# A fused two-block transformer kernel: order of gated products, sums, splits and row broadcasts

## The reference

```
h = rms_norm(x, norm1_g);  z = h @ w_in          # parts for three mixers and three gates
y = sigmoid(g_m)*(hm @ p_m) + sigmoid(g_a)*(ha @ p_a) + sigmoid(g_r)*(hr @ p_r)
x = x + y @ w_out
x = x + (silu(h2 @ w_gate) * (h2 @ w_up)) @ w_down
```

## Time and profile before

| | us | share of the span |
|---|---|---|
| median of 3 runs | 1624.04 | |
| profiled execution, span | 1618.2 | |
| TensorE (PE) busy | 1532.6 | 95% |
| weight loads (PEld) busy | 1163.6 | 72% |
| GpSimd (POOL) busy | 1261.5 | 78% |
| ScalarE (ACT) busy | 715.2 | 44% |
| VectorE (DVE) busy | 696.8 | 43% |

### The profile page before, as it was taken

How to read it: one execution, slowest core, us unless ns; L and a number is a source line. 1 busy time by engine, 2 the same in 40 slices (tenths; PEclk the granted TensorE clock), 3 DMA queues, 4 the chain that set the end, 5 groups by cost and what they waited for, 6 DMA issues and landing times.

```text
span 1618.2 us, 21936 instructions
## 1 busy us (share of the span) xinstructions
PE 1532.6 (95%) x7018; PEld 1163.6 (72%) x7018; DVE 696.8 (43%) x1306; ACT 715.2 (44%) x879; POOL 1261.5 (78%) x1509
## 2 busy tenths in 40 slices
PE   7989999999999999989999998999999899999996
PEld 5767877788887777777788776878785656646634
DVE  3986844300127986844210036355544122122215
ACT  4544543544446544534544445546341422325323
POOL 7997898999999996969999997977591634529713
PEclk9999999999999999999999999998999999999998
DMA  6654454677765553445677664645364988899990
GB/s 223 214 176 117 132 157 141 195 217 220 216 199 169 165 155 106 143 133 153 203 212 214 183 220 133 186 140 166 92 204 144 350 331 323 340 382 398 396 363 39
DMA packets 95525, 333.83 MB, mean 206 GB/s; under 512 B 11136, under 2 KB 15760, under 8 KB 94384
## 3 DMA queue, kind: packets, MB, share of 16 engines
q1 hardware_dynamic: 88240, 307.26, 58.1%
q10 hardware_dynamic: 6048, 21.22, 3.8%
q0 software_dynamic: 1152, 4.19, 0.7%
HBM read 322.12 MB, written 21.00 MB: 212 GB/s over the span
## 4 chain that ended last, share of the span: by engine, by line
POOL 53%; PE 27%; issue 15%; DMA 2%; DVE 1%; ACT 1%; POOLq 1%; ACTq 0%; DVEq 0%; SPq 0%
POOL w_lo L1835 52%; PE bank L671 7%; PE bank L1178 6%; PE bank L1232 3%; PE bank L1175 3%; PE bank L1198 3%; PE bank L1248 2%; PE bank L1288 1%; DMA logits<-outputs_by_expert,tiny 1%; DMA arena<-in_experts 1%; POOL w_lo L1842 1%; ACT w_hi L1402 1%; POOLq L1830 1%; PE bank L1218 0%; PE bank L1073 0%
## 5 line engine op out<-in xcount | busy, mean ns | idle before, releaser
L1835 POOL TENSOR_TENSOR w_lo<-raw,w_hi 128x256 fp32r<-128x256 f32 x1416 | 1067.6, 795 | 139.0 <-ACT w_hi L1402 138.0
L671 PE MATMUL bank<-w_hi,hT 128*128 128x512 f32 x2240 | 716.2, 401 | 39.4 <-POOL w_lo L1835 11.8
L1402 ACT ACTIVATE w_hi<-raw 128x1024 fp32r<-128x1024 f32 x371 | 393.0, 1059 | 545.6 <-DMA raw<-in_stream 291.0
L671 PEld LDWEIGHTS bank<-w_hi,hT 128*128 128x128 f32 x2240 | 417.4, 191 | 142.5 <-POOL w_lo L1835 19.9
L671 PE MATMUL bank<-w_lo,hT 128*128 128x512 f32 x1120 | 443.3, 396 | 0.0
L671 PEld LDWEIGHTS bank<-w_lo,hT 128*128 128x128 f32 x1120 | 213.9, 191 | 47.3
L1842 POOL TENSOR_TENSOR w_lo<-arena,w_hi 128x1024 fp32r<-128x1024 f32 x61 | 144.6, 2385 | 129.8 <-ACT w_hi L1402 129.7
L982 PE MATMUL bank<-w_hi,mixT 128*128 128x512 f32 x352 | 109.9, 393 | 1.0 <-POOL w_lo L1835 1.0
L671 PE MATMUL bank<-w_hi,mixT 128*128 128x512 f32 x288 | 91.6, 399 | 3.9 <-POOL w_lo L1835 2.6
L1402 ACT ACTIVATE w_hi<-arena 128x1024 fp32r<-128x1024 f32 x61 | 63.9, 1057 | 59.4 <-PE bank L1178 31.1
L2246 DVE SCALAR_TENSOR_TENSOR arena<-bank,tiny,arena 128x256 f32<-128x256 f32 x44 | 21.1, 483 | 155.5 <-ACT arena L1558 143.0
(11 more groups left out here) (392 smaller groups left out, 1928.3 us busy)
## 6 DMA issues: line engine op xcount, KB each, us to landing
raw<-in_stream SPq DMA_DIRECT2D x357, 512.0 KB, 3.6
arena<-in_experts SPq DMA_DIRECT2D x154, 512.0 KB, 11.1
raw<-in_experts SPq DMA_DIRECT2D x38, 512.0 KB, 9.5
rows_by_expert<-in_blank ACTq DMA_DIRECT2D x56, 128.0 KB, 3.3
arena<-in_stream SPq DMA_DIRECT2D x9, 512.0 KB, 13.2
gates<-rows_by_expert SPq DMA_DIRECT2D x3, 1024.0 KB, 7.7
outputs_by_expert<-xn ACTq DMA_DIRECT2D x3, 1024.0 KB, 8.4
bias_skewed<-bias_windows SPq DMA_DIRECT2D x4, 512.0 KB, 4.8
```

The costliest lines, as they stand in the source:

```text
L671: mm = pe.matmul(LIN[t][:, :], lhs[:, a, k0 + k, t * P:(t + 1) * P], w[:, k, :], start=(k0 + k == 0 and n == 0), stop=(k0 + k == nk - 1 an ...
L1402: act.activation(w_hi[:, s, :], src, ACT.Copy).then_inc(s_hi, 1)
L1835: part = nc.gpsimd.tensor_tensor(w_lo[:, i, c], raw[:, i, c], w_hi[:, i, c].bitcast(F32), ALU.subtract)
```

## The change

- `branch` with a sum becomes `added_branch`: both gated products (t = 0 and 1) come first, then both sums, then a wait of VectorE for itself; for the last two branches of y a small memset behind that wait gives the signal `s_nx` which the second sum gave. This concerns four branches in each layer and two in the second block, 20 sums.
- ScalarE's `unit()` with a feed has the order high, split, split, high.
- In `second()` VectorE splits both quarters' worth of tiles ahead of the products with g1.
- `seed()`, the zeros and GpSimd's operation for them are gone; the first matmul of each AB bank has `start=True`, and the wait for the banks stands behind `group()`.
- The four row broadcasts are spread: one ahead of the product, one behind each of its first three quarters.

```diff
-                for h in range(4):
-                    pe.matmul(ab_bank()[:, 0:SEQ], ident[0:4, h:h + 1].to_broadcast([4, P]), rows[:, 2, :], start=True,
-                              stop=True).then_inc(s_ab, 1)
-                product(hT, KT, "act")
+                def decay_row(h):
+                    if h < 4:
+                        pe.matmul(ab_bank()[:, 0:SEQ], ident[0:4, h:h + 1].to_broadcast([4, P]), rows[:, 2, :], start=True,
+                                  stop=True).then_inc(s_ab, 1)
+
+                decay_row(0)
+                product(hT, KT, "act", each=lambda q: decay_row(q + 1))
                 pe.wait_ge(s_act, acts.up())
...
-                seed()
                 group(between=lambda: hidden(TT))
-                down()
+                pe.wait_ge(s_ad, ab.back(0))
+                down(first=True)
...
-                            for a, w in ((0, hi), (1, hi), (0, lw)):
+                            for i, (a, w) in enumerate(((0, hi), (1, hi), (0, lw))):
                                 mm = pe.matmul(AB[2 * t + n][:, :], hidden_t[:, a, k, t * P:(t + 1) * P], w[:, k, :],
-                                               start=False, stop=True, skip_group_check=True)
+                                               start=(first and k == 0 and i == 0), stop=True, skip_group_check=True)
...
                     high()
                     split(dst, QK, gain, KT // 2)
+                    split(dst, QK, gain, KT // 2 + QK)
                     high()
-                    split(dst, QK, gain, KT // 2 + QK)
...
-            nc.gpsimd.tensor_scalar(zeros[:], ones[:, 0:P], 0.0, None, ALU.mult)
...
+            def added_branch(n_quarters, g, n, last=False):
+
+                def read(t):
+                    gt = gates[:, g, t, n * 512:(n + 1) * 512]
                     dve.tensor_tensor(tmpy[:, t, :], LIN[t][:, :], gt, ALU.mult).then_inc(s_ld, 1)
-                    dve.wait_ge(s_ld, ld.up())
-                    i = dve.scalar_tensor_tensor(y, tmpy[:, t, :], 1.0, y, ALU.mult, ALU.add)
-                    if last and t == 1:
-                        i.then_inc(s_nx, 1)
-                return read
+                    ld.up()
+
+                def add():
+                    dve.wait_ge(s_ld, ld.back(0))
+                    for t in range(TT):
+                        y = xn[:, t, n * 512:(n + 1) * 512]
+                        i = dve.scalar_tensor_tensor(y, tmpy[:, t, :], 1.0, y, ALU.mult, ALU.add)
+                    own(i)
+                    if last:
+                        dve.memset(tc(1003), 0.0).then_inc(s_nx, 1)
+
+                unit(n_quarters, read, add)
...
-                split(hT, QK, S_N1, KT // 2)
+                split(hT, KT // 2, S_N1, KT // 2)
                 for t in range(TT):
                     i = dve.tensor_tensor(xn[:, t, :], x[:, t, :], gain1, ALU.mult)
                 own(i)
-                split(hT, QK, S_N1, KT // 2 + QK)
```

More of the change, by code:

```diff
@@ L287, in program @@
         ones = sb("ones", [16, SEQ])
-        zeros = sb("zeros", [16, P], F32R)
         wexp = sb("wexp", [P, SLOTS, WIN])
@@ L949, in attention @@
                 return step, out
-            def seed():
-                pe.wait_ge(s_ad, ab.back(0))
-                for b in AB:
-                    pe.matmul(b[:, :], zeros[:], zeros[:, 0:1].to_broadcast([16, QC]), start=True, stop=False,
-                              skip_group_check=True)
             def hidden(later=0):
@@ L968, in group, with down @@
                 product(hT, KT, "dve", between=between)
-            def down(hidden_t=heT, halfway=None, between=None):
+            def down(hidden_t=heT, halfway=None, between=None, first=False):
                 pe.wait_ge(s_td, tr.back(0))
@@ L1826, in _ @@
             nc.gpsimd.memset(ones[:], 1.0).then_inc(s_z, 1)
-            pool.wait_ge(s_z, 1)
-            nc.gpsimd.tensor_scalar(zeros[:], ones[:, 0:P], 0.0, None, ALU.mult)
             nc.gpsimd.memset(mv[:, :, :, P:P + 1], 1.0).then_inc(s_z, 1)
@@ L1875, in _, with unit @@
             counts = [lin, pos, tr, th, ab, ad, std, exps, la, ld, g, pv, smc, rs, first, own]
-            def unit(n, read=None):
+            def unit(n, read=None, after=None):
                 v = lin.up()
@@ L1886, in unit @@
                 read(1)
+                if after:
+                    after()
             def col(at, i=0):
@@ L2213, in two_heads, with branch @@
                 return (qlatA if j < 2 else qlatB)[:, 2 * (j % 2):2 * (j % 2) + 2, :].rearrange("p a t -> p (a t)")
-            def branch(g, n, first=False, last=False):
+            def branch(g, n):
                 def read(t):
                     y, gt = xn[:, t, n * 512:(n + 1) * 512], gates[:, g, t, n * 512:(n + 1) * 512]
-                    if first:
-                        dve.tensor_tensor(y, LIN[t][:, :], gt, ALU.mult).then_inc(s_ld, 1)
-                        ld.up()
-                        return
-                    dve.tensor_tensor(tmpy[:, t, :], LIN[t][:, :], gt, ALU.mult).then_inc(s_ld, 1)
-                    dve.wait_ge(s_ld, ld.up())
-                    i = dve.scalar_tensor_tensor(y, tmpy[:, t, :], 1.0, y, ALU.mult, ALU.add)
-                    if last and t == 1:
-                        i.then_inc(s_nx, 1)
-                return read
+                    dve.tensor_tensor(y, LIN[t][:, :], gt, ALU.mult).then_inc(s_ld, 1)
+                    ld.up()
+                return read
+            def added_branch(n_quarters, g, n, last=False):
+                def read(t):
+                    gt = gates[:, g, t, n * 512:(n + 1) * 512]
+                    dve.tensor_tensor(tmpy[:, t, :], LIN[t][:, :], gt, ALU.mult).then_inc(s_ld, 1)
+                    ld.up()
+                def add():
[7 more added lines that the diff above has]
+                unit(n_quarters, read, add)
             def residual(n):
@@ L2346, in layer @@
                 dve.wait_ge(s_la, la.up(8))
-                unit(2, branch(0, 0, first=True))
-                unit(2, branch(0, 1, first=True))
+                unit(2, branch(0, 0))
+                unit(2, branch(0, 1))
                 dve.wait_ge(s_exp, exps.up())
                 row_stat(ALU.add)
-                unit(2, branch(1, 0))
+                added_branch(2, 1, 0)
                 over_sum()
@@ L2355, in layer @@
                 attend_latent()
-                unit(2, branch(1, 1))
+                added_branch(2, 1, 1)
                 dve.wait_ge(s_la, la.up(4))
-                unit(2, branch(0, 0, last=True))
+                added_branch(2, 0, 0, last=True)
                 split(hT, KT // 2)
-                unit(2, branch(0, 1, last=True))
+                added_branch(2, 0, 1, last=True)
                 split(hT, KT // 2, None, KT // 2)
@@ L2761, in yb_scaled @@
                     return dve.tensor_scalar(v, v, tc(32, 2 * t + g), None, ALU.mult)
-                gated = branch(0, 0, first=True)
+                gated = branch(0, 0)
                 def gated_and_scaled(t):
@@ L2774, in second @@
                 split(mixT8, KT // 2, S_NS)
-                unit(2, branch(0, 1, first=True))
+                unit(2, branch(0, 1))
                 split(mixT8, KT // 2, S_NS, KT // 2)
-                unit(4, branch(1, 0, last=True))
+                added_branch(4, 1, 0, last=True)
                 dve.wait_ge(s_th, th.up())
@@ L2781, in second @@
                 split(hT, KT // 2)
-                unit(4, branch(1, 1, last=True))
+                added_branch(4, 1, 1, last=True)
                 split(hT, KT // 2, None, KT // 2)
```

## The result

The changed kernel took 1649.49 us in the median of 4 runs (1645.2 to 1655.83), the kernel before 1626.11 us in 4 runs beside it (1620.61 to 1632.1): a ratio of 1.0162, 95% interval 1.0125 to 1.0198. That is 26 us slower by the ratio, where 5 us faster was forecast. The profiled execution of the changed kernel took 1655.83 us with a span of 1654.0, 35.8 more than the span of before.

A forecast was written before the change was run, and what follows sets the result against it. TensorE and GpSimd were taken to bound the kernel at equal pace, coupled by a ring of three quarters. +2.0 - 3.8 - 3.7 + 0.3 = -5.2 gave a span of 1613.0 and a median of 1619 us, range 1611.5 to 1628.5.

The forecast's parts named there:

- Part E: Row broadcasts spread over the quarters ahead of the mLSTM: the stretch gets 1.0 us longer a layer, +2.0 in all.
- the quarters: The four quarters with the spread broadcasts: they end earlier, so the mLSTM scores come 1.9 us earlier a layer.
- VectorE's tail: VectorE's masks and wide sum behind the last broadcast: 6.2 us, ending late, with TensorE waiting about 3.5 us.
- rival 3: Half clock stays behind the broadcasts or returns through TensorE's new 3.5 us wait: +1.7 us a layer, chance 0.17.
- the four's half clock: TensorE at half clock for 3.4 us behind the four broadcasts: costs 1.7 us a layer, taken as gone when spread.
- Part A: Gated products ahead of sums: TensorE no longer waits for a long sum in layer 1, -3.8 us once.
- it hangs on the sums now being asked for where the second sums were: Condition for the -3.8 us of products ahead of sums: one first sum of twenty was long, median 1.11 us.
- Rival 2: A long first sum returns and delays TensorE through over_sum: median 1628, or 1638 in both layers; chance 0.15 (0.03 both).
- B and C: Earlier splits at the start of the second block: TensorE's 4.29 us wait and half clock there go, -3.7 us.
- D: No zero products in each layer: TensorE waits longer for VectorE's residual L2246 by as much, 0 us.

The follow-up runs named there:

- e_only: The kernel before with only the four row broadcasts spread, one ahead of the product and one behind each of its first three quarters: ratio 1.0100.
- d_only: The kernel before with only the zeros (`seed()` and GpSimd's operation for them) gone: ratio 0.9995.
- a_only: The kernel before with only `added_branch`, both gated products ahead of the sums: ratio 1.0056.

## Why the prediction was wrong

**Part E, +2.0 forecast, +16 measured (1.0100).** Its three terms, a layer of the changed kernel: the quarters gained 0.4 and not 1.9, because a single broadcast among full products costs 3.57 - 2.72 = 0.85 us and not the 0.48 that it has in a row of four. VectorE's tail came out late as I had it, but from a start 1.1 us later and with 7.05 us in place of 6.2 (L2328 3.77 in place of 3.36, the first mask 0.92 for 0.56): TensorE's wait was 3.89, forecast 3.5. And the half clock came behind that wait. In the sum it stood at nothing; rival 3 had it, at 1.7 us, half of the 3.4 us of the other half clock. That was the mis-sized term: it lasted 10.3 us in this place, and the step 37-38, +7.9, is 3.2 of longer wait and 4.7 of slow clock. In e_only it lasted 6.8 us and the step grew by 6.4, 3.2 of them slow clock. So about half of the time at the low level is lost, as I had it; what didn't carry over from one place to another is how long the level stays low. The 1.7 us that I booked for the four's half clock were no gain either, for the reason found above: TensorE would have waited for GpSimd in that time.

**Part A, -3.8 forecast, +9 measured (1.0056).** The step that failed is "it hangs on the sums now being asked for where the second sums were". I took 6.30 us as one long one of twenty. Across seven profiles with the old order and no pauses the first sum of branch(1, 0) takes either 0.78 to 0.81 or 6.28 to 6.30 us, never anything between: 6 times of 7 the long one in layer 1, once in layer 0. It is bounded, because the waiting sum holds back the next gated product, that holds TensorE, TensorE holds ScalarE, and GpSimd runs out of work 3.8 us later, which lets the sum through. The wait that A removes is what ended the starvation. That this chain lets it through is argued from the equal lengths. In the new order three of four first sums were long, 5.17, 7.90 and 10.55 us. Rival 2 had this mechanism, the 3.8 us and nearly the wait; its chance, 0.15 and 0.03 for both layers, was taken from a median that counted eighteen sums at other places. The row of twelve parts back to back was the evidence, and I had it.

**The 7.6 us at the end of layer 1** in the changed kernel are the same thing in another instruction, L2279 with 8 columns, 9.84 us. I saw L2273 at 4.04 and did not carry it into the sum. It is no part's own: d_only has it there, a_only in layer 0, the others don't.

**B and C, -3.7 forecast.** Against the profile of before the stretch 290-300 fell by 3.5 to 3.9, as forecast; against the mean of the profiles without B and C it fell by 0.6. In the timing nothing is left (1.0007), as the forecast was made against one execution whose transfer was late. The step that failed is taking the 4.29 us as a property of the kernel.

**D, 0 forecast.** Right: 0.9995, and TensorE's wait for the residual grew from 1.0 to 2.0 us each.

**The four broadcasts' half clock**: right that spreading ends it, wrong that it costs 1.7 us. Pairs, which I hadn't considered, gain 1.2 us a layer by another way and cost no tail.

## What to carry to other kernels

Before you take away a wait, ask what it holds back besides its own engine: here it was the only thing that stopped GpSimd, and so the bound on a starvation elsewhere. Spread work only as far as its last reader has slack, and price a drop of the clock by the stretch that follows the new wait, and only where no other engine would have held TensorE in that time. One profile of before is one draw: a stall in it that hangs on a transfer's arrival is worth less than it shows, which a second profile of any neighbouring kernel tells for nothing.

## What the runs showed of the hardware

- An instruction of VectorE with both tensors in SBUF can wait over many parts of GpSimd: 10.55 us over some 14 parts of 0.7 us, and 9.84 us for one of 8 columns. The Trainium skill (SBUF — State Buffer, "Who interferes with whom") has the loser blocked for the one whole instruction that has the shared port pair. Most sums agree with it (19 of the 20 in the profile of before took 0.69 to 1.22 us); the long ones do not. With pauses of 0.16 us behind every four parts no sum took over 1.31 us. With one of the two inputs from PSUM, 60 sums in three kernels took 0.69 us each.
- It goes the other way as well: a part of GpSimd that came behind a VectorE sum of 3.36 us took 3.34 us and not 0.7.
- TensorE fell to the 1.2 GHz level behind four broadcasts with 4 rows each, though it was never idle, at ten of sixteen places, and behind pairs or single ones at none. Every idle time of 3.89 us and longer that began at the 2.4 GHz level was followed by the fall too, or had it inside; shorter ones went either way (3.10 us in a_only at 988.15 was followed by it, 3.09 at the start of the second block after was not).
- A single 4-row broadcast between full products costs TensorE 0.85 us, four in a row 0.5 each.
